# Feed-forward products of a two-block kernel: each weight tile loaded twice instead of three times, with two sums side by side in a PSUM bank

## The chip, the cores and the metric

The kernel runs on one core of a Trainium2 chip. The metric is the device time of one execution in microseconds (us); the figure used is the median of several runs. Engines are named as in the profile: TensorE (PE, its weight loads PEld), VectorE (DVE), ScalarE (ACT), GpSimd (POOL) and SyncE (SP), which issues the weight loads from memory.

## What is computed

Two transformer blocks run one after the other on 256 rows of 1024 features (the first block has 16 more rows, which no longer count when its feed-forward part begins). Both end in a feed-forward part, and these are what the change touches:

```python
# first block: gate and up are 1024 x 2816, down is 2816 x 1024
h = h + (jax.nn.silu(hn @ w_gate[l]) * (hn @ w_up[l])) @ w_down[l]
# second block: up is 1024 x 4096, down is 4096 x 1024
x = x + jnp.square(jax.nn.relu(h2 @ w_up[l])) @ w_down[l]
```

`hn` and `h2` are the RMS-normed rows. Everything is float32.

## The kernel before, in words

**Split numbers.** TensorE multiplies a reduced float format (fp32r) at full speed. To keep the accuracy, every operand x is held as two parts, the first x rounded to the format and the second the rest, x minus the first. A product is then three matmuls: first x first, first x second, and second x first. `three` (lines 524 to 530) issues them into one PSUM region. For weights as the stationary side these are three weight loads (a, a, b) and three streams of the rows (c, d, c).

**Pieces.** The weights come as a list of 251 pieces, most 128 x 1024 (512 KB), in the order of `PIECES`. SyncE loads piece i into one of five slots of `raw` as soon as piece i-5 has been split. ScalarE copies it into the first part (line 1320, `first_parts`), VectorE subtracts (line 1843, `second_parts`), and the two parts lie in one of six slots of `parts`, free again when TensorE has used the piece six before. This is called a split below.

**The order of VectorE and ScalarE.** All engines have one written order. `full` and `freed` (waits for a bank to be filled, or emptied) first call `keep_ahead`: before an engine waits for a bank, it does its share of the splits up to the fourth piece (`AHEAD = 4`) behind the last piece that went into this bank. So the splits stand between the waits for the banks, and a late wait makes all splits behind it late.

**First block's feed-forward part** (lines 913 to 926). For each of 22 feature tiles f, TensorE computes gate.f into columns 0 to 255 of a PSUM bank and up.f into columns 256 to 511 (`feature_product`, 8 weight tiles k of 128 features for each, 24 matmuls of 256 columns). One bank, `gu_f`, holds both; four banks take turns. After f = 0 it also multiplies out `rows2`, the inverse norms of the rows for all partitions, which wait for VectorE's `rms2`. After f = 5, 9, 13 and 17 it does four pieces of down (`down`, lines 863 to 902: 12 matmuls of 512 columns for each piece, into banks 4 to 7), and after f = 21 the last six, in two rounds, one for each tile of rows. VectorE (line 2135 on) multiplies the bank by the inverse norms into `gu` (line 2138) and then, in `hidden_rest`, waits for ScalarE's SiLU (line 1523), multiplies gate and up (2131), waits for ScalarE's copy into the first part of the hidden tile (1525), and subtracts for the second part (2133). down for tiles f-5 to f-2 waits for these.

**Second block's** (lines 1263 to 1276). 32 pieces of up, two to a bank (`up_j`, j = 0 to 15); from j = 3 on, after every second j, four pieces of down. ScalarE applies ReLU straight from the bank (line 1742) into one of four `relu2` slots, squares it into the first part (1744), and GpSimd squares again and subtracts (1811, 1813). VectorE has nothing but splits here, from the end of the norm (line 2544) to the last results (line 2550).

Of the kernel before, what the change touches and what calls it, by code (L numbers as in the profile page):

```python
# [150 lines left out]
def build(nc, consts, params, weights, x, meta, out, line_dram):  # L151
    ctx = ExitStack()
    with ctx:
# [137 lines left out]
        def release(ins, name):  # L291
            ins.then_inc(bank_free[jobs[name][0]], 1)
# [193 lines left out]
        def _(pe):  # L486
# [44 lines left out]

            arrivals = {}
# [16 lines left out]
            def feature_product(name, cols, ps, acts=hT, ahead_of={}):  # L549

                w = [half.rearrange("p (k n) -> p k n", k=KD) for half in split(name)]
                for k in range(KD):
                    if k in ahead_of:
                        ahead_of[k]()
                    need(k)
                    last = three(ps, [h[:, k, :] for h in w], [acts[:, s, k, cols] for s in range(2)],
                                 k == 0, k == KD - 1)
# [355 lines left out]
            for f in range(FT1):  # L913
                name = f"gu_{f}"
                ps = opened(name)
                done_with(f"gate.{f}", feature_product(f"gate.{f}", tok, ps[:, 0:SEQ],
                                                       ahead_of={4: lambda: first_rows(1)} if f == 0 else {}))
                if f == 0:
                    turn[0], turn[1] = 0, 4
                closed(feature_product(f"up1.{f}", tok, ps[:, SEQ:2 * SEQ]), name)  # L920
                piece_used[f"up1.{f}"] = name
# [341 lines left out]
            for n in range(8):  # L1263
                for j in (2 * n, 2 * n + 1):
                    name = f"up_{j}"
                    ps = opened(name)
                    done_with(f"up2.{2 * j}", feature_product(f"up2.{2 * j}", tok, ps[:, 0:SEQ],
                                                              ahead_of=late_rows if j == 0 else {}))
                    if j == 0:
                        turn[0], turn[1] = 0, 4  # L1270
                    closed(feature_product(f"up2.{2 * j + 1}", tok, ps[:, SEQ:2 * SEQ]), name)
                    piece_used[f"up2.{2 * j + 1}"] = name
# [30 lines left out]
        def _(act):  # L1303
# [216 lines left out]
            for f in range(FT1):  # L1520
                full(act, f"gu_{f}")
                freed(act, f"gu_{f}")
# [213 lines left out]
            for j in range(FT2 // 2):  # L1736
                name = f"up_{j}"
                full(act, name)
                if j >= 4:

                    act.wait_ge(sem("hidden2"), j - 3)
                release(A(relu2[:, j % 4, :], bank_of(name), ACT.Relu), name)
                freed(act, name)
# [74 lines left out]
        def _(dve):  # L1818
# [317 lines left out]
            for f in range(FT1):  # L2136
                full(dve, f"gu_{f}")
# [587 lines left out]
```

## Time and profile before

| | |
|---|---|
| median of 3 runs | 939.38 us (938.78 to 940.14) |
| profiled execution | 939.0 us |
| its span, first to last instruction | 937.2 us |
| mean granted clock of TensorE | 0.996 |
| busy: TensorE, VectorE, ScalarE, GpSimd | 98%, 66%, 50%, 17% |
| first feed-forward part | about 153.7 to 343 us of the span |
| second feed-forward part | about 752 to 935 us |

The busy share of TensorE counts the time in which any matmul is under way. Matmuls overlap in the array (one of 256 columns lasts 0.28 us, but the next starts 0.12 us after it), so the cost of one is read from the distance between starts. A timeline row gives start, duration, engine, line, operation, tiles and count, and in brackets how long the engine was idle before it and for whom it waited.

### The profile page before, as it was taken

What the parts mean: (1) busy time and instruction counts of PE and PEld (TensorE: products, weight loads), DVE (VectorE), ACT (ScalarE), POOL (GpSimd) and SP (SyncE); (2) the same over time, 40 slices, a digit from 0 to 9 for tenths busy, and PEclk for the clock granted to TensorE, in tenths of its full rate; (3) what the DMA queues carried; (4) which work ended last, traced back from release to release, by engine and by line L of the source; (5) the groups of instructions that cost most, each with busy time, mean ns of one, the idle gap of its engine ahead of it and who ended that gap; (6) DMA issues with size and microseconds to landing.
All of it is one profiled execution on the core that took longest, in us unless ns stands there. A gap on an engine that the chain in (4) does not pass through costs nothing. (4 is left out here: it accounts for less than half of the span.)

```text
span 937.2 us, 17705 instructions
## 1 busy us (share of the span) xinstructions
PE 921.7 (98%) x6958; PEld 827.6 (88%) x6958; DVE 616.3 (66%) x1335; ACT 466.3 (50%) x925; POOL 155.3 (17%) x111
## 2 busy tenths in 40 slices
PE   9999999999999999999999999999999999999998
PEld 8898787999999989888988888998888899999996
DVE  4657767657556587799777878356775674555543
ACT  6555655545445364474444773354453464444441
POOL 1100000000000007002974214000000023332231
PEclk9999999999999999999999999999999999999999
DMA  6830343565556444655432101032746545555551
GB/s 246 265 130 1 101 142 117 166 217 179 181 181 218 161 156 156 222 178 188 152 117 86 46 14 69 3 115 69 237 138 208 180 138 201 180 181 191 192 179 45
DMA packets 38579, 139.31 MB, mean 149 GB/s; under 512 B 4326, under 2 KB 4582, under 8 KB 38497
## 3 DMA queue, kind: packets, MB, share of 16 engines
q1 hardware_dynamic: 37152, 134.10, 43.3%
q10 hardware_dynamic: 816, 2.25, 0.7%
q0 software_dynamic: 528, 1.84, 0.6%
q8 instruction: 55, 0.90, 0.4%
q14 instruction: 28, 0.22, 0.1%
HBM read 137.09 MB, written 1.08 MB: 147 GB/s over the span
## 5 line engine op out<-in xcount | busy, mean ns | idle before, releaser
L1843 DVE TENSOR_TENSOR parts<-raw,parts 128x1024 fp32r<-128x1024 f32 (+2 forms) x225 | 285.2, 1303 | 128.7 <-ACT parts L1320 123.8
L1320 ACT ACTIVATE parts<-raw 128x1024 fp32r<-128x1024 f32 (+2 forms) x225 | 228.1, 1050 | 117.5 <-PE psum L530 97.2
L528 PE MATMUL psum<-hT,parts 128*128 128x256 f32 (+1 forms) x928 | 263.9, 284 | 1.4 <-DVE hT L1860 1.2
L529 PE MATMUL psum<-hT,parts 128*128 128x256 f32 (+1 forms) x928 | 262.5, 283 | 0.0
L530 PE MATMUL psum<-hT,parts 128*128 128x256 f32 (+1 forms) x928 | 260.9, 281 | 0.0
L528 PEld LDWEIGHTS psum<-hT,parts 128*128 128x128 f32 x928 | 174.7, 188 | 5.0 <-issue 1.8
L530 PEld LDWEIGHTS psum<-hT,parts 128*128 128x128 f32 x928 | 176.0, 190 | 0.0
L529 PEld LDWEIGHTS psum<-hT,parts 128*128 128x128 f32 x928 | 175.0, 189 | 0.5
L528 PE MATMUL psum<-parts,arena_r 128*128 128x512 f32 x344 | 135.1, 393 | 0.9 <-DVE arena_r L1858 0.7
L530 PE MATMUL psum<-parts,arena_r 128*128 128x512 f32 x344 | 134.0, 390 | 0.0
L529 PE MATMUL psum<-parts,arena_r 128*128 128x512 f32 x344 | 133.9, 389 | 0.0
L1369 ACT ACTIVATE arena<-arena,npeaks 128x128 f32<-128x128 f32 (+4 forms) x136 | 55.9, 414 | 50.0 <-DVE npeaks L1921 20.1
L528 PEld LDWEIGHTS psum<-parts,arena_r 128*128 128x128 f32 x344 | 64.6, 188 | 14.6 <-DVE arena_r L1858 1.4
L530 PEld LDWEIGHTS psum<-parts,arena_r 128*128 128x128 f32 x344 | 64.6, 188 | 13.6
L529 PEld LDWEIGHTS psum<-parts,arena_r 128*128 128x128 f32 x344 | 64.6, 188 | 12.5
L528 PE MATMUL psum<-parts,hT 128*128 128x512 f32 (+1 forms) x176 | 69.2, 393 | 1.7 <-DVE peaks L1921 1.1
L1774 POOL TENSOR_SCALAR arena<-cbuf 128x256 f32<-128x256 f32 x16 | 16.8, 1049 | 320.5 <-DVE scr L2169 319.4
L529 PE MATMUL psum<-parts,hT 128*128 128x512 f32 (+1 forms) x176 | 68.1, 387 | 0.0
L530 PE MATMUL psum<-parts,hT 128*128 128x512 f32 (+1 forms) x176 | 68.0, 387 | 0.0
L1811 POOL TENSOR_TENSOR arena<-arena 128x512 f32<-128x512 f32 x16 | 17.2, 1073 | 284.1 <-ACT arena_r L1744 284.1
L1784 POOL TENSOR_TENSOR parts<-raw,parts 128x1024 fp32r<-128x1024 f32 x20 | 48.5, 2422 | 1.6
L647 PE MATMUL psum<-arena 128*128 128x128 f32 x288 | 40.1, 276 | 1.4 <-DVE arena L2336 1.0
(329 smaller groups left out, 1192.9 us busy)
## 6 DMA issues: line engine op xcount, KB each, us to landing
raw<-weights SPq DMA_DIRECT2D x247, 512.0 KB, 4.1
raw<-weights SPq DMA_DIRECT2D x4, 384.0 KB, 4.4
X<-x SPq DMA_DIRECT2D x2, 512.0 KB, 5.2
out<-X SPq DMA_DIRECT2D x2, 512.0 KB, 2.6
arena<-lines POOLq DMA_DIRECT2D x1, 768.0 KB, 9.8
cbuf<-consts ACTq DMA_DIRECT2D x1, 561.0 KB, 6.5
arena<-lines POOLq DMA_DIRECT2D x1, 544.0 KB, 5.9
arena<-params ACTq DMA_DIRECT2D x1, 512.0 KB, 6.5
```

Of the source, the lines that this page charges most:

```text
L528: mm(ps, a, c, start=start, stop=False)
L529: mm(ps, a, d, start=False, stop=False)
L530: return mm(ps, b, c, start=False, stop=stop)
L647: last = mm(o, flat[:, at:at + P], vt[t], start=(t == 0 and not g["meta"]), stop=(t == g["tiles"] - 1))
L1320: signal(A(split_slot(name)[0], whole_piece, ACT.Copy), "first_parts")
L1369: signal(A(map_slot(g, E, n), map_slot(g, S, n), ACT.Exp, bias=npeaks[:, col:col + 1], scale=-1.0 if negated else 1.0, accum_out=sums[:, c ...
L1774: nc.gpsimd.tensor_scalar(al[:, h, :], cst("negdist"), slope, None, ALU.mult).then_inc(sem("alibi"), 1)
L1784: nc.gpsimd.tensor_tensor(second, whole_piece, first.bitcast(F32), ALU.subtract)\
L1811: nc.gpsimd.tensor_tensor(v, v, v, ALU.mult).then_inc(sem("squares2"), 1)
L1843: signal(V_.tensor_tensor(second, whole_piece, first.bitcast(F32), ALU.subtract), "split_vector")
```

## The change

`side_by_side` replaces `three` where the region given is a whole bank of 512 columns. The stationary side is the first part of the weights once, with both parts of the rows as one moving operand (512 columns, two sums side by side), and the second part of the weights once, with the first part of the rows (256 columns, added to the left sum). The wanted product is the sum of the two halves. Each gate, up1 and up2 piece now fills a bank of its own. In the first block VectorE adds the halves of each bank with a reduction over groups of two (step 256) into `gu`, and then multiplies by the inverse norms there. In the second block VectorE adds them into `relu2`, and ScalarE's ReLU works in place. Down and all other products stay as they are. The waits follow: ScalarE waits for `rows_scaled` instead of the bank, and the slot of `relu2` is waited for by VectorE.

```diff
+            def side_by_side(ps, stationary, moving, start, stop):
+
+                a, b = stationary
+                two_sums = ps.rearrange("p (s n) -> p s n", s=2)
+                if start:
+                    mm(two_sums, a, moving, start=True, stop=False)
+                    return mm(ps[:, 0:SEQ], b, moving[:, 0, :], start=False, stop=False)
+                mm(ps[:, 0:SEQ], b, moving[:, 0, :], start=False, stop=False)
+                return mm(two_sums, a, moving, start=False, stop=stop)
...
-                    last = three(ps, [h[:, k, :] for h in w], [acts[:, s, k, cols] for s in range(2)],
-                                 k == 0, k == KD - 1)
+                    if ps.shape[-1] == 2 * SEQ:
+                        last = side_by_side(ps, [h[:, k, :] for h in w], acts[:, :, k, cols], k == 0, k == KD - 1)
+                    else:
+                        last = three(ps, [h[:, k, :] for h in w], [acts[:, s, k, cols] for s in range(2)],
+                                     k == 0, k == KD - 1)
...
             for f in range(FT1):
-                name = f"gu_{f}"
-                ps = opened(name)
-                done_with(f"gate.{f}", feature_product(f"gate.{f}", tok, ps[:, 0:SEQ],
-                                                       ahead_of={4: lambda: first_rows(1)} if f == 0 else {}))
-                if f == 0:
-                    turn[0], turn[1] = 0, 4
-                closed(feature_product(f"up1.{f}", tok, ps[:, SEQ:2 * SEQ]), name)
-                piece_used[f"up1.{f}"] = name
+                for w, piece in enumerate((f"gate.{f}", f"up1.{f}")):
+                    name = f"gu{w}_{f}"
+                    ps = opened(name)
+                    closed(feature_product(piece, tok, ps,
+                                           ahead_of={4: lambda: first_rows(1)} if f == w == 0 else {}), name)
+                    piece_used[piece] = name
+                    if f == w == 0:
+                        turn[0], turn[1] = 0, 4
...
-                full(act, f"gu_{f}")
-                freed(act, f"gu_{f}")
+                full(act, f"gu1_{f}")
+                act.wait_ge(sem("rows_scaled"), f + 1)
...
             for j in range(FT2 // 2):
-                name = f"up_{j}"
-                full(act, name)
-                if j >= 4:
-
-                    act.wait_ge(sem("hidden2"), j - 3)
-                release(A(relu2[:, j % 4, :], bank_of(name), ACT.Relu), name)
-                freed(act, name)
+                full(act, f"up1_{j}")
+                freed(act, f"up0_{j}")
+                freed(act, f"up1_{j}")
+                signal(A(relu2[:, j % 4, :], relu2[:, j % 4, :], ACT.Relu), "relu2")
+                act.wait_ge(sem("relu2"), j + 1)
...
             for f in range(FT1):
-                full(dve, f"gu_{f}")
-                release(V_.tensor_tensor(ffn1["gu"].rearrange("p (s n) -> p s n", s=4)[:, f % 4, :], bank_of(f"gu_{f}"),
-                                         ffn1["rows"], ALU.mult), f"gu_{f}")
+                for w in range(2):
+                    name = f"gu{w}_{f}"
+                    full(dve, name)
+                    release(V_.tensor_reduce(gu[:, f % 4, w, :], bank_of(name).rearrange("p (s n) -> p n s", s=2), AXX,
+                                             ALU.add), name)
+                freed(dve, f"gu0_{f}")
+                freed(dve, f"gu1_{f}")
+                both_rows = ffn1["gu"].rearrange("p (s n) -> p s n", s=4)[:, f % 4, :]
+                signal(V_.tensor_tensor(both_rows, both_rows, ffn1["rows"], ALU.mult), "rows_scaled")
                 hidden_rest(f)
...
+            for j in range(FT2 // 2):
+                for w in range(2):
+                    name = f"up{w}_{j}"
+                    full(dve, name)
+                    if j >= 4 and w == 0:
+                        dve.wait_ge(sem("hidden2"), j - 3)
+                    release(V_.tensor_reduce(relu2[:, j % 4, SEQ * w:SEQ * w + SEQ],
+                                             bank_of(name).rearrange("p (s n) -> p n s", s=2), AXX, ALU.add), name)
```

The part of TensorE's loop over the second block's pieces changes as the first block's does, with banks `up0_j` and `up1_j` in place of `up_j`.

## Rows read from the trace of the kernel before

**Rows 1.** The page, part 1: busy time, share of the span, instructions.

```profile
PE 921.7 (98%) x6958; PEld 827.6 (88%) x6958; DVE 616.3 (66%) x1335; ACT 466.3 (50%) x925; POOL 155.3 (17%) x111
```

**Rows 2.** Windows inside both feed-forward parts: length, engines' busy time, clock, DMA.

```profile
162.99:202.40 39.41, 39.41 (x291) 37.57 (x290) 27.21 (x34) 21.42 (x30) 0.00 (x0) 1.00 0.58 185
202.40:236.10 33.70, 33.70 (x242) 31.82 (x241) 20.43 (x24) 15.07 (x20) 0.00 (x0) 1.00 0.58 193
760.00:788.50 28.50, 28.50 (x198) 26.63 (x197) 20.27 (x20) 15.60 (x19) 13.33 (x8) 1.00 0.58 186
788.50:910.00 121.50, 121.50 (x806) 112.11 (x805) 61.32 (x43) 56.15 (x65) 34.77 (x22) 1.00 0.57 186
```

**Rows 3.** Groups of TensorE by form: busy us, mean ns, idle before.

```profile
L528 PE MATMUL psum<-parts,arena_r 128*128 128x512 f32 x344 | 135.1, 393 | 0.9 <-DVE arena_r L1858 0.7
L528 PE MATMUL psum<-parts,hT 128*128 128x512 f32 x152 | 61.0, 401 | 0.6 <-DVE parts L1843 0.3 <-DVE hT L2181 0.2
```

**Rows 4.** Timeline of ScalarE, two of its copies during down pieces.

```profile
233.74 1.06 ACT L1320 ACTIVATE parts<-raw 128x1024 fp32r<-128x1024 f32 x1 [1.66 <-PE psum L530]
236.46 1.06 ACT L1320 ACTIVATE parts<-raw 128x1024 fp32r<-128x1024 f32 x1 [1.66 <-PE psum L530]
```

**Rows 5.** Timeline of VectorE, one steady gate/up pair.

```profile
247.81 0.69 DVE L2138 TENSOR_TENSOR arena<-psum,arena 128x512 f32<-128x512 f32 x1 [0.25 <-PE psum L530]
249.04 0.43 DVE L2131 TENSOR_TENSOR arena<-arena 128x256 f32<-128x256 f32 x1 [0.54 <-ACT arena L1523]
250.90 2.36 DVE L1843 TENSOR_TENSOR parts<-raw,parts 128x1024 fp32r<-128x1024 f32 x2 [0.52 <-ACT parts L1320]
253.51 0.69 DVE L2138 TENSOR_TENSOR arena<-psum,arena 128x512 f32<-128x512 f32 x1 [0.25 <-PE psum L530]
```

**Rows 6.** Timeline of VectorE at the first pairs of the first block.

```profile
163.97 0.69 DVE L2138 TENSOR_TENSOR arena<-psum,arena 128x512 f32<-128x512 f32 x1 [0.23 <-ACT arena L1518]
...
168.34 2.36 DVE L1843 TENSOR_TENSOR parts<-raw,parts 128x1024 fp32r<-128x1024 f32 x2 [0.53 <-ACT parts L1320]
170.61 0.69 DVE L2138 TENSOR_TENSOR arena<-psum,arena 128x512 f32<-128x512 f32 x1
...
173.70 2.36 DVE L1843 TENSOR_TENSOR parts<-raw,parts 128x1024 fp32r<-128x1024 f32 x2 [0.53 <-ACT parts L1320]
175.98 0.68 DVE L2138 TENSOR_TENSOR arena<-psum,arena 128x512 f32<-128x512 f32 x1
```

**Rows 7.** Groups of VectorE by form.

```profile
L2138 DVE TENSOR_TENSOR arena<-psum,arena 128x512 f32<-128x512 f32 x22 | 15.2, 690 | 16.5 <-PE psum L530 16.3 <-ACT arena L1518 0.2
...
L2151 DVE TENSOR_TENSOR arena<-X,arena 128x512 f32<-128x512 f32 x4 | 2.8, 692 | 0.1
...
L2292 DVE TENSOR_REDUCE st<-arena 128x16 f32<-128x1024 f32 x1 | 1.2, 1214 | 0.0
```

**Rows 8.** Timeline of VectorE at the end of the first block.

```profile
326.63 0.69 DVE L2138 TENSOR_TENSOR arena<-psum,arena 128x512 f32<-128x512 f32 x1 [0.25 <-PE psum L530]
...
330.06 2.36 DVE L1843 TENSOR_TENSOR parts<-raw,parts 128x1024 fp32r<-128x1024 f32 x2 [0.58 <-ACT parts L1320]
...
334.61 0.68 DVE L1901 TENSOR_TENSOR X<-psum,X 128x512 f32<-128x512 f32 x1
335.33 0.69 DVE L2151 TENSOR_TENSOR arena<-X,arena 128x512 f32<-128x512 f32 x1
```

**Rows 9.** Timeline of TensorE, the first matmul of gate.1.

```profile
162.99 0.36 PE L528 MATMUL psum<-hT,parts 128*128 128x256 f32 x1
```

**Rows 10.** Timelines of ScalarE, VectorE and GpSimd, start of the second block.

```profile
760.70 0.60 ACT L1742 ACTIVATE arena<-psum 128x512 f32<-128x512 f32 x1 [0.93 <-PE psum L530]
...
777.82 0.60 ACT L1742 ACTIVATE arena<-psum 128x512 f32<-128x512 f32 x1 [2.54 <-PE psum L530]
...
762.95 3.96 DVE L1843 TENSOR_TENSOR parts<-raw,parts 128x1024 fp32r<-128x1024 f32 x2 [0.24 <-ACT parts L1320]
...
763.68 2.15 POOL L1813 TENSOR_TENSOR arena_r<-arena,arena_r 128x512 fp32r<-128x512 f32 x1
```

More of the change, by code:

```diff
@@ L1264, in _ @@
                 for j in (2 * n, 2 * n + 1):
-                    name = f"up_{j}"
[L1266 to L1272, printed above, removed]
+                    for w in range(2):
+                        name = f"up{w}_{j}"
+                        piece = f"up2.{2 * j + w}"
+                        ps = opened(name)
+                        closed(feature_product(piece, tok, ps, ahead_of=late_rows if j == w == 0 else {}), name)
+                        piece_used[piece] = name
+                        if j == w == 0:
+                            turn[0], turn[1] = 0, 4
                 if n >= 1:
@@ L1736, in _ @@
             for j in range(FT2 // 2):
-                name = f"up_{j}"
-                full(act, name)
-                if j >= 4:
-                    act.wait_ge(sem("hidden2"), j - 3)
-                release(A(relu2[:, j % 4, :], bank_of(name), ACT.Relu), name)
-                freed(act, name)
+                full(act, f"up1_{j}")
[3 more added lines that the diff above has]
+                act.wait_ge(sem("relu2"), j + 1)
                 signal(A(a2[:, 0, 2 * j:2 * j + 2, :], relu2[:, j % 4, :], ACT.Square), "hidden2_first")
@@ L2544, in _ @@
             link(V_.tensor_tensor(st[:, 10:12], st[:, 4:6], st[:, 4:6], ALU.mult))
+            for j in range(FT2 // 2):
+                for w in range(2):
+                    name = f"up{w}_{j}"
+                    full(dve, name)
[3 more added lines that the diff above has]
+                                             bank_of(name).rearrange("p (s n) -> p n s", s=2), AXX, ALU.add), name)
             for t in range(TT):
```

## The prediction, as it was made before the changed kernel ran

> **What bounds the kernel now.** I read the busy shares and slices of the page first, then the matmul groups by form, then, for the stretches that the change touches, the timelines of VectorE and ScalarE. TensorE is busy 98% of the span, VectorE 66% [rows 1]. Both feed-forward stretches show TensorE busy without a gap, with a granted clock of 1.00, its 2.4 GHz level [rows 2], so a cheaper stream of matmuls shortens the span, unless another engine then sets the pace.
>
> What a matmul costs is its distance to the next. A gate/up pair (48 matmuls of 256 columns) takes 5.70 us: two VectorE products that each waited for TensorE stand at 247.81 and 253.51 [rows 5], so 118.8 ns each, where 256 columns at 2.4 GHz are 106.7. One down piece (12 matmuls of 512) takes 2.72 us, from the two splits on ScalarE that wait for TensorE at 233.74 and 236.46 [rows 4]: 226.7 ns for 213.3 of columns. A matmul with its weights thus costs about 12 to 13 ns beside its columns, wide or narrow.
>
> VectorE has hardly any room in a gate/up pair. There it does two splits (128x1024), one product (512) and two small ones (256) with two waits for ScalarE between them; the steady pair of 5.70 us has 0.25 us of waiting for TensorE in it [rows 5]. In the first pairs of the first block it starts late and never waits for TensorE: 170.61 to 175.98 is a pair of 5.37 us [rows 6].
>
> **The change part by part.** *Matmuls.* Per weight tile k three matmuls of 256 become one of 512 and one of 256: 356.3 becomes 226.7 + 118.8 = 345.5 ns, 10.8 less. There are 44 + 32 pieces of 8 tiles, 608 in all: 6.6 us; per pair 0.17 (5.70 to 5.53). The bounds: the 512-wide matmuls whose stationary side is hT are longer in the list (401 against 393 ns [rows 3]); 8 ns more on each would leave 1.7 us of the 6.6. Here the stationary side is `parts`, so I take 226.7. The upper bound is a switch of weights that costs nothing behind a wide matmul: 12 ns more on each of 608, 7 us; every narrow and wide row carries the same extra, so I don't expect it. The Trainium skill ("TensorE: Matmul & The Clock Gate", Back-to-back issue gap) gives N/2.4 + 2.5 ns for the gap; by that a matmul less is worth 2.5 ns and the whole edit 1.5 us. The trace disagrees with it: 12 ns, so its rule is not in my sum.
>
> *VectorE, first block.* Each pair gains two reductions of 512 elements from PSUM, and the product with the rows stays, now from SBUF and behind its own engine's semaphores. The trace has no reduction with groups of two and a step of 256 between the two. Nearest: 512 elements take 690 ns from PSUM and 692 from SBUF, and a reduction of 1024 with long groups 1214 ns [rows 7], that is 1.02 ns for each further element, the rate of the other operations. I take 0.69. The lower bound is the 256-wide operation, as if only the outputs counted (0.42 [rows 5]; each 0.27 less per reduction takes 0.54 from VectorE's pair, and the first and the last wait below all but vanish: 3 us more gained). The upper bound is each element counting twice, the 1024-wide row (1.22). Back to back a 512-wide operation occupies 0.60 (the next starts before its end), behind a wait on itself 0.72 (334.61 to 335.33 [rows 8]). VectorE's pair becomes 5.37 + 0.60 + 0.72 = 6.69 us, against 5.53 of TensorE. It falls back 1.16 us in every pair and catches up only while TensorE works on the four down pieces (10.88 us, in which VectorE has four splits of 1.14 to do). A cycle of four pairs and four down pieces is 31.3 us for VectorE and 33.0 for TensorE, so it catches up wholly, if nothing overflows before.
>
> Does it overflow? VectorE's order is written: it splits the piece four ahead of the bank's last piece before it waits for that bank. Call R(f) the start of the emptying of gate.f.
> At the start: TensorE waits for the inverse rows and starts gate.1 at 162.99 as now [rows 9]. VectorE's first product stands at 163.97 because ScalarE's copy of the rows ends then; two reductions come ahead of it, 1.32 later. The split at 168.34 moves to 169.66 and R(1) is 170.80. R(4) = 190.87, R(5) = 197.56. TensorE ends up.5 at 162.99 + 5 x 5.53 = 190.64. The banks (four, reused after four pieces) are just free: gate.5 wants bank 2 at 185.1, emptied at R(3) + 0.75 = 184.9. Split down.0 stands ahead of R(4), ready 191.0 (0.3 late); split down.2 ahead of R(5), ready 197.7, wanted at 191.0 + 5.44 = 196.4 (1.2 late); split gate.6 follows the whole of step 5, R(5) + 0.60 + 1.14 + 0.72 + 3.09 + 1.23 = 204.3, wanted 203.1 (1.2 late). Now gate.6 starts at 162.99 + 5 x 5.70 + 10.88 = 202.4. So the first six pairs end 1.9 us later than now, and how fast the matmuls are does not matter there.
> In the middle, pairs 6 to 21: nothing is late, 16 x 0.17 = 2.8 us gained.
> At the end pairs 18 to 21 run without down pieces; R(18) can stand 3.0 after gate.18 starts (its 2.77 and the end of the last matmul), R(21) 20.1 later, and the split of down.20, which stands behind step 21, is ready at 23.1 + 5.55 + 1.23 = 29.8. TensorE wants it at 4 x 5.53 + 4 x 1.36 = 27.6: 2.2 us of waiting. Now that split ends at about 331.2 [rows 8], 4.6 after the product of 326.63, and TensorE wants it 5.4 after. First block: 1.9 - 2.8 + 2.2 = 1.3 us longer. ScalarE's SiLU, copy and splits only move with VectorE.
>
> *Second block.* VectorE gets two reductions per pair; the ReLU reads SBUF instead of PSUM (a 128x512 row either way), the square and GpSimd's two operations keep their order. Here VectorE had only splits, about 2.3 us per pair, lengthened by GpSimd (two take 3.96 at 762.95 [rows 10]). A new chain arises: ReLU behind the second reduction, then square, then ScalarE's next split, then VectorE's: 760.70 to 762.95 now [rows 10], so 2.25. VectorE's pair: 1.14 + 0.60 + 1.14 + 0.72 + 2.25 = 5.9, and up to 7.0 with GpSimd's 1.1, against 5.53. From 761.5 on (where the norm's chain ends now) the first pair brings VectorE to 766.2, three more to 783.8 or, at 7.0 each, to 787.2, and the split of up2.8 is ready between 785.0 and 789.4; TensorE wants it at 788.0 in the new pace and has it at 788.5 in the old (777.82 + 10.88, less ScalarE's 0.2 behind the last matmul [rows 10]). I count these four pairs as no gain. The other 12 have down pieces between them (VectorE 19 us of 22) and gain 12 x 0.17 = 2.1 us. ReLU slots, hidden tiles and the end of the block have a pair and more to spare.
>
> **Sum.** 1.3 - 2.1 = -0.8 us on the profiled execution's 939.0 us (span 937.2): 938.2. The median of the runs shown is 0.4 above that execution, so 938.6. About 0.2% (1.9 us) is what a measurement of this kernel can tell from no change; my forecast lies within it.
>
> **The rivals.** *A, the reduction is slow.* Its two operands lie 256 words apart, so every read jumps. By the upper bound (1.22, back to back 1.14, behind a wait 1.25) VectorE's pair is 7.76 us and R(1) 171.9. Then gate.6 is split at 171.9 + 4 x 7.76 + 7.8 = 210.7, 8.3 later than it starts now; a cycle (4 x 7.76 + 4 x 1.14 = 35.6) is 1.9 longer than TensorE's present one (33.7), three times, 5.7; at the end down.20's split comes 4.4 + 3 x 7.76 + 7.8 = 35.5 after gate.18, wanted after 28.3 in the present pace, 7.2; in the second block four pairs make up2.8 4.4 late, less the 2.1, 2.3. Together 23.5, 962 us; half way, at 0.95 us, 950. It decides from about 0.90 us on, where VectorE's cycle passes TensorE's. For it: no row has a jump at each element. Against it: VectorE's forms cost their element count alone [rows 7]. The Trainium skill has both: "Advanced Engine Details and Errata", PSUM Cachelines, wants every two consecutive elements adjacent; "Vector Engine (DVE) Microarchitecture Reference", Measured stream behaviour on trn2, has 1.73 ns per element for a two-source operation that jumps every element (an estimate of 1.04 us for this one, 954 us), but the full rate for a one-source operation that alternates between two regions of SBUF and writes one word for two read, which is the shape of this one. No row here shows either. Chance 0.25: 950 us, 944 to 962.
> *B, VectorE keeps up.* If my three waits don't arise (TensorE's pieces are buffered deeper than I count, or VectorE's waits for ScalarE shrink when it is late), the 6.6 us come in, less the first pair of each block, where TensorE waits for the norm: 933.3. For it: VectorE is busy only 50 to 71% of these stretches [rows 2]. Against it: the written order, and the 5.37 us pair that had no wait for TensorE. Chance 0.12.
> *C, the saving per matmul is mostly absent* (1.7 us or less of it): of the 28 pairs that I count as gained each brings 0.04 instead of 0.17, and the last wait shrinks by as much: 941; inside my own range.
>
> **How the numbers follow.** Forecast 0.63, A 0.25, B 0.12. The forecast's own range is 936.0 to 942. The range has to take in part of A: 936.0 to 955 leaves out about 0.11 below (B) and 0.09 above. Faster by over 0.2% (under 937.5): B and 0.06 of the forecast, 0.18. Within: 0.44. Slower (over 941.3): A, and 0.13 of the forecast, 0.38.
>
> **What would show it.** Reductions of 0.69 us on VectorE, 76 of them. Pairs of 5.53 us in the middle of both blocks. VectorE's pair at 6.7 us from 171 to 197, no wait for TensorE in it; TensorE waiting for VectorE's splits (line of the subtraction) about 2.7 us in all before gate.6 and 2.2 at the last down pieces, nowhere else over 1 us. The forecast is wrong if a reduction takes over 0.90 us, if waits for splits appear in the cycles 6 to 17, or if there are none at all.

## The result, and the profile after

| | before | after |
|---|---|---|
| median of the runs on one chip (5 each) | 940.14 us (938.78 to 941.30) | 949.46 us (947.20 to 951.52) |
| profiled execution, its span | 939.0, 937.2 us | 949.46, 947.6 us |
| mean granted clock of TensorE | 0.996 | 0.994 |

The change makes the kernel slower: 1.0096 times the time before, 95% interval 1.0081 to 1.0111. The forecast was 938.6 us and no measurable change. 949.5 lies inside the stated range (936 to 955), but outside the forecast's own (936.0 to 942). That it lies inside is luck: the range reached so far up for the slow reduction of rival A, and the reductions were not slow.

The page of the changed kernel, part 1, stands against [rows 1]:

```profile
PE 924.7 (98%) x6350; PEld 799.7 (84%) x6350; DVE 656.1 (69%) x1411; ACT 465.3 (49%) x925; POOL 154.5 (16%) x111
```

TensorE issues 608 matmuls and 608 weight loads fewer, as written. It is nevertheless busy 3 us longer, and the span has grown by 10.4 us. VectorE has 76 more operations and 40 us more work.

The windows of the changed kernel (length, busy time of PE, PEld, DVE, ACT and POOL with counts, PEclk, DMA share, GB/s) stand against [rows 2]; two short ones are added:

```profile
162.99:202.40 39.41, 37.77 (x195) 32.30 (x196) 28.93 (x41) 16.03 (x24) 0.00 (x0) 0.96 0.46 137
165.54:168.90 3.36, 3.36 (x12) 2.88 (x12) 1.43 (x3) 1.70 (x2) 0.00 (x0) 0.50 0.36 138
339.60:343.00 3.40, 3.40 (x9) 2.62 (x9) 2.83 (x4) 0.90 (x1) 0.00 (x0) 0.50 0.81 258
788.50:910.00 121.50, 121.50 (x607) 102.64 (x606) 77.58 (x69) 59.98 (x70) 38.44 (x24) 1.00 0.56 194
```

In the first window TensorE now has gaps (37.77 of 39.41 us busy), and its clock is 0.96. The two short windows are stretches at the 1.2 GHz level (0.50), one right after each of the two long waits below. In the last window the engine has no gap and the full clock, as before.

To say where the time went, I compare the start of the same work on TensorE in both traces (after less before, us of the span):

| point | after less before | added since the row above |
|---|---|---|
| first feed-forward part begins (same code up to here) | +0.6 | +0.6 |
| gate.6 begins | +3.8 | +3.2 |
| pairs 6 to 21 done | +3.7 | -0.1 |
| down of the first block done | +8.9 | +5.2 |
| before the products of the compressed keys, about 388 us | +9.9 | +1.0 |
| second feed-forward part begins | +10.6 | +0.7 |
| end | +10.4 | -0.2 |

So two places cost 8.4 us between them, and the 5 us that the forecast expected from cheaper matmuls in the middle and in the second block did not come. The 0.6, 1.0 and 0.7 lie in code that the change does not touch. The 1.0 comes and goes without it: e6, which is the kernel before with one buffer moved, has 1.5 us there.

**The first place: gate.1.** Timeline of TensorE of the changed kernel (start, duration, engine, line, operation, tiles; in brackets the idle time and for whom it waited):

```profile
163.16 0.71 PE L917 MATMUL psum<-cbuf,st 128*128 128x128 f32 x4 [0.70 <-DVE st L1886]
165.34 0.68 PE L537 MATMUL psum<-hT,parts 128*128 128x512 f32 x1 [1.47 <-DVE arena L2151]
165.82 0.41 PE L538 MATMUL psum<-hT,parts 128*128 128x256 f32 x1
166.04 0.41 PE L539 MATMUL psum<-hT,parts 128*128 128x256 f32 x1
166.25 0.63 PE L540 MATMUL psum<-hT,parts 128*128 128x512 f32 x1
166.68 0.41 PE L539 MATMUL psum<-hT,parts 128*128 128x256 f32 x1
```

The first matmul of gate.1 waits 1.47 us for a reduction of VectorE (line 2151). gate.0 was put into bank 2, where the rotation stood. Then the rotation is reset, up.0 gets bank 0, `rows2` bank 1, and gate.1 bank 2 again, before VectorE has emptied it. The half clock follows: the wide matmul of 166.25 has its successor 0.43 us later, where at full clock it is 0.23. From the first matmul of gate.1 to that of gate.6 the changed kernel takes 1.5 us more than before.

**The second place: down.20.** Timelines of TensorE and VectorE of the changed kernel:

```profile
335.38 0.39 PE L530 MATMUL psum<-parts,arena_r 128*128 128x512 f32 x1
339.12 0.47 PE L528 MATMUL psum<-parts,arena_r 128*128 128x512 f32 x1 [3.35 <-DVE parts L1854]
339.42 0.49 PE L529 MATMUL psum<-parts,arena_r 128*128 128x512 f32 x1
339.72 0.63 PE L530 MATMUL psum<-parts,arena_r 128*128 128x512 f32 x1
340.14 0.63 PE L528 MATMUL psum<-parts,arena_r 128*128 128x512 f32 x1
```

```profile
310.40 0.69 DVE L2151 TENSOR_REDUCE arena<-psum 128x256 f32<-128x512 f32 x1 [0.90 <-PE psum L540]
...
313.25 0.69 DVE L2151 TENSOR_REDUCE arena<-psum 128x256 f32<-128x512 f32 x1 [1.03 <-PE psum L540]
...
318.29 0.68 DVE L2151 TENSOR_REDUCE arena<-psum 128x256 f32<-128x512 f32 x1
...
320.81 0.69 DVE L2156 TENSOR_TENSOR arena<-arena 128x512 f32<-128x512 f32 x1
322.04 0.43 DVE L2142 TENSOR_TENSOR arena<-arena 128x256 f32<-128x256 f32 x1 [0.55 <-ACT arena L1536]
322.95 0.42 DVE L2144 TENSOR_TENSOR arena_r<-arena,arena_r 128x256 fp32r<-128x256 f32 x1 [0.48 <-ACT arena_r L1538]
323.90 1.23 DVE L1854 TENSOR_TENSOR parts<-raw,parts 128x1024 fp32r<-128x1024 f32 x1 [0.53 <-ACT parts L1333]
325.05 0.68 DVE L2151 TENSOR_REDUCE arena<-psum 128x256 f32<-128x512 f32 x1
...
335.84 0.42 DVE L2142 TENSOR_TENSOR arena<-arena 128x256 f32<-128x256 f32 x1 [0.82 <-ACT arena L1536]
...
337.75 2.36 DVE L1854 TENSOR_TENSOR parts<-raw,parts 128x1024 fp32r<-128x1024 f32 x2 [0.58 <-ACT parts L1333]
```

In pairs 18 to 21, without down pieces between them, VectorE needs 6.76 us a pair (318.29 to 325.05) and TensorE 5.7. No operation of that pair waits for TensorE, and the waits for ScalarE in it (0.55, 0.48, 0.53) are those of the pair before the change (0.54, 0.48, 0.52 or 0.53; two of them in [rows 5]): the pair is longer by VectorE's own added operations. The split of down.20 starts at 337.75 and lets TensorE go on at 339.12; before the change it was ready at about 331.2 [rows 8].

**The middle.** The changed kernel's matmuls within one piece (the distance between starts is the cost):

```profile
274.03 0.28 PE L539 MATMUL psum<-hT,parts 128*128 128x256 f32 x1
274.15 0.40 PE L540 MATMUL psum<-hT,parts 128*128 128x512 f32 x1
274.39 0.28 PE L539 MATMUL psum<-hT,parts 128*128 128x256 f32 x1
274.50 0.39 PE L540 MATMUL psum<-hT,parts 128*128 128x512 f32 x1
274.73 0.28 PE L539 MATMUL psum<-hT,parts 128*128 128x256 f32 x1
...
275.90 0.42 PE L540 MATMUL psum<-hT,parts 128*128 128x512 f32 x1
276.15 0.29 PE L539 MATMUL psum<-hT,parts 128*128 128x256 f32 x1
```

The narrow matmul costs 0.11 to 0.12 us. The wide ones cost 0.24, 0.23 and 0.25. Over the pieces of 225 to 292 us the medians for the wide one are 231, 228, 256 and 233 ns as k goes up, repeating every four k, 237 on average; the narrow one is at 119.5. A weight tile costs 356.4 ns (2853 a piece), and before it cost 356.5. Of the 10.8 ns a tile that the forecast counted on, 0.1 came.

### The profile page after: what moved, and what is told of

Its sections match the earlier page's. It is cut to its first block and busy times, and to the rows that moved or that the text cites. A ratio compares the mean times of both kernels' runs of the same rounds, so it can differ in the third digit from the quotient of the medians.

```text
span 947.6 us, 16642 instructions
## 1 busy us (share of the span) xinstructions
PE 924.7 (98%) x6350; PEld 799.7 (84%) x6350; DVE 656.1 (69%) x1411; ACT 465.3 (49%) x925; POOL 154.5 (16%) x111
## 5 line engine op out<-in xcount | busy, mean ns | idle before, releaser
L1854 DVE TENSOR_TENSOR parts<-raw,parts 128x1024 fp32r<-128x1024 f32 (+2 forms) x225 | 280.2, 1275 | 85.9 <-ACT parts L1333 80.3
L540 PE MATMUL psum<-hT,parts 128*128 128x512 f32 x532 | 194.6, 402 | 0.0
L539 PE MATMUL psum<-hT,parts 128*128 128x256 f32 x532 | 151.2, 284 | 1.2 <-DVE hT L1871 1.2
L540 PEld LDWEIGHTS psum<-hT,parts 128*128 128x128 f32 x532 | 101.2, 190 | 22.5
L539 PEld LDWEIGHTS psum<-hT,parts 128*128 128x128 f32 x532 | 100.9, 190 | 5.6 <-DVE hT L1871 1.7
L528 PE MATMUL psum<-hT,parts 128*128 128x256 f32 (+1 forms) x320 | 92.7, 290 | 0.2 <-DVE parts L1854 0.2
L529 PE MATMUL psum<-hT,parts 128*128 128x256 f32 (+1 forms) x320 | 91.2, 285 | 0.0
L530 PE MATMUL psum<-hT,parts 128*128 128x256 f32 (+1 forms) x320 | 90.7, 283 | 0.0
L528 PEld LDWEIGHTS psum<-hT,parts 128*128 128x128 f32 x320 | 60.8, 190 | 2.9 <-issue 1.8
```

Of the source, the lines that this page charges most:

```text
L528: mm(ps, a, c, start=start, stop=False)
L529: mm(ps, a, d, start=False, stop=False)
L530: return mm(ps, b, c, start=False, stop=stop)
L539: mm(ps[:, 0:SEQ], b, moving[:, 0, :], start=False, stop=False)
L540: return mm(two_sums, a, moving, start=False, stop=stop)
L1854: signal(V_.tensor_tensor(second, whole_piece, first.bitcast(F32), ALU.subtract), "split_vector")
```

## The experiments

Ratios are against runs of the kernel before on the same chip, with 95% intervals.

**e1_narrow: the wide matmul taken apart again.** Does the saved weight load bring anything?

```diff
                 mm(ps[:, 0:SEQ], b, moving[:, 0, :], start=False, stop=False)
-                return mm(two_sums, a, moving, start=False, stop=stop)
+                if stop:
+                    return mm(two_sums, a, moving, start=False, stop=True)
+                mm(ps[:, 0:SEQ], a, moving[:, 0, :], start=False, stop=False)
+                return mm(ps[:, SEQ:2 * SEQ], a, moving[:, 1, :], start=False, stop=False)
```

> Changed kernel, but in 6 of the 8 weight tiles of each gate, up1 and up2 piece (k = 1 to 6) the 512-wide matmul is issued as two of 256, so the first part of the weights is loaded twice again: three loads as before, the sum the same. Theory (the wide matmul is worth no more than two narrow ones here; in the changed kernel it costs 228 to 256 ns by k, 238 on average, and two narrow ones of the kernel before cost 117.8 + 121): a gate/up pair stays at 5.70 us and the time at the changed kernel's, 949.5 +- 1.5. Rival (a saved load does bring the 10.9 ns per tile that the prediction took, and something else of the change eats it): pairs of 5.83 us, 456 x 10.9 ns = 5 us more, 954.5.

Measured: 947.81 us, ratio 1.0073 (1.0057 to 1.0088), 1.7 us under the changed kernel's 949.46 (the intervals of the two ratios overlap), where the rival had 5 us more. The bank wait, the wait at down.20 and both stretches at half clock are there again. A piece costs 2833 ns where the changed kernel's costs 2853: each of the six tiles taken apart became some 3 ns cheaper, and 76 pieces of 20 ns are 1.5 us. As the kernel stands, one wide matmul thus costs slightly more than two narrow ones with a load of their own. Why it does, this run does not say; e7 does.

**e2_bank: another rotation.** up.0 goes into bank 3, so that gate.1 does not meet bank 2.

```diff
                     if f == w == 0:
-                        turn[0], turn[1] = 0, 4
+                        turn[0], turn[1] = 3, 4
...
+            turn[0] = 44
             down("down1", FT1 - 6, 6, "d1", FT1, aT, hidden1, first_tile_turned)
```

> Changed kernel, but the banks of the first block's loop are taken from bank 3 on instead of bank 0 on, so that gate.1 doesn't take bank 2, which holds gate.0 until VectorE has emptied it (the bank of the later stages is set back to what it was). Theory (TensorE waits 1.5 us at gate.1 for that bank, and the wait brings a stretch of 3.4 us at half clock, 1.5 us more; without it VectorE, whose pair takes 6.76 us against 5.70, is what TensorE meets next): no wait at gate.1 and no half clock there, but waits for splits between down.0 and gate.6, whose start goes from 206.3 to about 205.4 (when VectorE has split it); about 1 us gained, 948.5. Rival (VectorE is not late enough for that): the whole 3.2 us come back, 946.3, gate.6 at 203.1.

Measured: 947.28 us, 1.0069 (1.0054 to 1.0084), between the two expectations; the trace decides between them. The wait at gate.1 and the half clock behind it are gone. In their place come waits for VectorE's splits at down.2 and gate.6. Timeline of TensorE of e2:

```profile
197.71 0.50 PE L528 MATMUL psum<-parts,arena_r 128*128 128x512 f32 x1 [0.90 <-DVE parts L1855]
204.57 0.47 PE L537 MATMUL psum<-hT,parts 128*128 128x512 f32 x1 [1.11 <-DVE parts L1855]
```

These are the waits that the prediction had worked out (1.2 and 1.2). The changed kernel hid them behind its bank wait. The changed kernel's bank wait is thus real, but little is to be had by taking it away, since VectorE's lateness lies right behind it: from the start of the part to gate.6 e2 loses 2.4 us against the kernel before, and the changed kernel 3.2. The rest of the 2.2 us between e2 and the changed kernel lies in code that they share (in the traces 1.0 us before the part begins and 0.9 ahead of the compressed keys).

**e3_early: the splits of down.20 and down.21 ahead of step 21.**

```diff
+                if f == FT1 - 1:
+                    second_parts(INDEX[f"down1.{f}"] + 1)
                 freed(dve, f"gu0_{f}")
                 freed(dve, f"gu1_{f}")
```

(The same on ScalarE, and the rotation set to 22 for what comes later.)

> Changed kernel, but in the last step of the first block (f = 21) both engines do their shares of the splits of down.20 and down.21 ahead of the product with the rows and the SiLU, instead of behind the whole step; the banks of the later stages are counted on from 22, as in the kernel before. Theory (TensorE waits 3.5 us for the split of down.20, and loses 1.7 us more in the 3.4 us at half clock that follow): both gone, 5.2 us gained, 944.3. Rival (the hidden tile 21 or the norm's chain, now 2.3 us later on VectorE, take its place): a new wait of 1 to 3 us before down.21 or before the norm's products, 946 to 949. And if the later banks matter, the 0.9 us longer wait before the compressed keys (about 388 us) goes too, else not.

Measured: 950.23 us, 1.0094 (1.0078 to 1.0111): nothing gained. The wait for the split turns into one for the last hidden tile. Timeline of TensorE of e3:

```profile
341.34 0.53 PE L528 MATMUL psum<-parts,arena_r 128*128 128x512 f32 x1 [1.86 <-DVE arena_r L2147]
```

Half clock follows this wait too. The stage costs 3.8 us more than before, where the changed kernel's costs 5.2, and the new rotation adds 1.6 us of bank wait at the start of the second block. One operation put first makes another late: what is late there is VectorE's whole queue.

**e4_pair512: both parts of a row tile stored as one run of 512 words.**

```diff
+        hF = hT[:, :, :, :].rearrange("p s k n -> p (s k n)")[:, 0:2 * KD * SEQ].rearrange("p (k s n) -> p s k n", s=2, k=KD)
...
-                    closed(feature_product(piece, tok, ps,
+                    closed(feature_product(piece, tok, ps, acts=hF,
```

> Changed kernel, but the rows of both feed-forward parts lie in hT so that the two parts of a feature tile k are side by side (512 words in one run, starting every 2 KB, instead of two runs of 256 that lie 8704 bytes apart and start every 1088 bytes). Theory (the wide matmul's cost goes by where its rows lie: 231, 228, 256, 233 ns for k mod 4 = 0 to 3 in the changed kernel): 227 ns for each k, and the narrow one 117 for each: a pair of 5.50 us; 3.2 us gained in pairs 6 to 21, 2.5 in the second block, and the wait at down.20 takes some 0.5 of it back: 944. Rival (a moving operand from hT costs 6 ns more whatever its place): pairs of 5.60, 946.5. Third (no effect of layout): 949.5.

Measured: 946.37 us, 1.0059 (1.0043 to 1.0076). The wide matmuls come out at 229 to 240 ns, 234 on average, without the 256; a weight tile at 352. It lies between the two expectations and pointed on: in down, 512 columns of `parts` as the moving side take 227. `hT` starts at byte 100704 of a partition, an odd multiple of 32, and `parts`, by the sizes declared between the two, at a multiple of 128.

**e5_second_only: the change in the second block alone.** (The hunks of the first block left out.)

> The kernel before with the change made in the second feed-forward block alone. Theory (the saved weight load is worth nothing, and the loss sits at two places of the first block: the bank wait and half clock at gate.1, 3 us, and the late splits, their wait and half clock at the end of the first block, 5 us): the time of before within 1.5 us, 939 to 941.5, second block within 0.5 us of before's (its k tile about 356 ns). Rival (the change costs or gains something in the second block that the traces hide, such as VectorE arriving late at the down pieces there): more than 2 us from before, either way.

Measured: 942.54 us, 1.0024 (1.0013 to 1.0036), 1 us above the expectation. In the trace there is one new wait at the beginning of the second feed-forward part. Timeline of TensorE of e5:

```profile
765.48 0.50 PE L537 MATMUL psum<-hT,parts 128*128 128x512 f32 x1 [1.61 <-DVE arena L2562]
```

up_0's first bank is 1, the reset gives the third sum bank 1 again: the same mistake as at gate.1, and here only because the first block leaves the rotation elsewhere. A stretch of 3.4 us at half clock at 483 us accounts for 1.7 us more of the profiled execution. From 777 us to the end the second part runs 0.1 us faster than before. So the second part gains nothing, and loses nothing but this bank wait, which the fully changed kernel does not have; that kernel's loss is in the first block.

**e6_before_moved: the kernel before, with `hT` on a boundary.** One declaration moves; no instruction changes.

```diff
+        scr = sb("scr", [P, 514])
         hT = sb("hT", [P, 2, KD, ALL], F32R)
...
-        scr = sb("scr", [P, 514])
```

> The kernel before with one SBUF buffer (scr, 2056 bytes a partition) declared ahead of hT and not behind it, so that hT starts at a multiple of 64 and 128 bytes in its partition (102784) instead of at an odd multiple of 32 (100704); arena_r keeps its place; no instruction changes. Theory (a moving operand off a 64-byte boundary costs 3 to 6 ns a matmul): the three 256-wide matmuls of a k tile fall from 117.8, 121 and 117.8 ns, the 512-wide ones on hT from about 233 to 227; over the 608 weight tiles of the feed-forward blocks alone 1 to 6 us less, 934 to 939. Rival (the place in SBUF is nothing to TensorE): same time within 0.7 us and the same pitches.

Measured: 939.91 us, 0.9991 (0.9979 to 1.0003). The weight tile falls from 356.5 to 355.0 ns, which over 608 tiles is 0.9 us. The expectation of 3 to 6 ns for each matmul was too high: 256-wide matmuls hardly feel the place. Down's matmuls, neither of whose operands moves, meanwhile cost 227.6 ns instead of 226.8, which takes nearly the same back. The 0.7 us by which the median is lower are not clear of noise.

**e7_after_moved: the changed kernel, with the same move.**

> The changed kernel with the same move of scr ahead of hT. Theory (place): the two-run matmuls fall from 231, 228, 256 and 233 ns by k mod 4 toward 227 in all, the k tile from 356 to 345 ns; the middle and the second block gain 3 to 5 us, 944 to 947, while VectorE's splits become the limit in the first block. Rival 1 (the two runs of 256 words cost it, not where they start): the pattern by k stays and the time stays at 949 to 950. Rival 2 (only the outlier at one k in four goes): k tile 350 ns, 947 to 948.

Measured: 945.69 us, 1.0062 (1.0044 to 1.0081). Timeline of TensorE of e7, one piece up to k = 4:

```profile
271.10 0.39 PE L537 MATMUL psum<-hT,parts 128*128 128x512 f32 x1
271.33 0.28 PE L538 MATMUL psum<-hT,parts 128*128 128x256 f32 x1
271.44 0.28 PE L539 MATMUL psum<-hT,parts 128*128 128x256 f32 x1
271.56 0.39 PE L540 MATMUL psum<-hT,parts 128*128 128x512 f32 x1
271.78 0.28 PE L539 MATMUL psum<-hT,parts 128*128 128x256 f32 x1
271.90 0.40 PE L540 MATMUL psum<-hT,parts 128*128 128x512 f32 x1
272.13 0.28 PE L539 MATMUL psum<-hT,parts 128*128 128x256 f32 x1
```

The wide matmul now costs 0.22 to 0.23 us at nearly every k (medians 226 to 235), the piece 2780 ns, the weight tile 347.5: 9 ns less than in the kernel before. From 624 us to 911 us the kernel gains 2.2 us, 0.1 of it ahead of the second part, so that the part has the 2.1 of the forecast, and pairs 6 to 21 gain 2.2. This settles the missing saving. The other side grows at the same time. The window of e7 behind its wait:

```profile
335.88:341.00 5.12, 5.12 (x12) 4.07 (x13) 4.13 (x5) 1.56 (x3) 0.00 (x0) 0.51 0.74 244
```

and the waits of its TensorE (us in total, times, longest):

```profile
PE psum L528 <- DVE parts L1854: 4.5, 3, 3.7
...
PE psum L537 <- DVE parts L1854: 1.1, 1, 1.1
```

TensorE is faster, so VectorE is late by more: 3.7 us at down.20, and 1.1 at gate.6. The clock fell to half within the wait and stays there for 5 us behind it.

**e8_pair_moved: e4's layout and the move together.**

> The changed kernel with both rows of parts stored as one run of 512 words for each k (as e4) and with the move of scr ahead of hT. Theory (place and runs both cost): 512-wide at 227, narrow 117.8, k tile 345 ns as the forecast had it; against e4 (946.4) 2 us less in the second block and up to 1 us in the first, where VectorE is then late at the down pieces: 943 to 945.5. Rival (the 234 ns of e4 is the price of this matmul wherever the rows lie): no different from e4, 946 to 947.

Measured: 945.01 us, 1.0056 (1.0037 to 1.0075), pieces of 2812 and 2777 ns in turn, a weight tile of 349.3. The expected 345 is not reached, and in time e7 and e8 can't be told apart. The wide matmul stays where e4 had it, 234 ns on average: in this layout the move brings 2 to 3 ns a tile, nearly all of it in the narrow one, where with the kernel's own layout it brought 9. So the start of `hT` is not all that counts, and what else does, no run shows. With `hT` in place, two runs of 256 words cost nothing over one of 512.

**e9_half_read: a lighter VectorE in the first block.** The sum of the right half of each bank is left out.

```diff
-                    release(V_.tensor_reduce(gu[:, f % 4, w, :], bank_of(name).rearrange("p (s n) -> p n s", s=2), AXX,
-                                             ALU.add), name)
+                    release(V_.tensor_tensor(gu[:, f % 4, w, :], bank_of(name)[:, 0:SEQ], ffn1["rows"][:, SEQ * w:SEQ * w + SEQ],
+                                             ALU.mult), name)
...
-                signal(V_.tensor_tensor(both_rows, both_rows, ffn1["rows"], ALU.mult), "rows_scaled")
```

> e7 (the changed kernel, hT moved to a 128-byte boundary) with VectorE's three operations on a first-block pair (two reductions of 0.68 us and the product of 0.69 us) replaced by two products of 256 words that read the left half of each bank alone: the right half's sum is left out, TensorE's work is unchanged. Theory (the losses of the first block are VectorE's pair of 6.76 us, which falls to some 5.6 us): the wait of about 3.5 us at down.20 and the bank and split waits at gate.1, down.2 and gate.6 shrink to under 0.5 us in all and the half-clock stretch after the end goes with its wait; 940 to 941 goes to e7's 945.7 less 5 to 8 us: 937.5 to 940.5. Rival (the wait at the end is the pair's new chain through ScalarE, not VectorE's load): the end wait stays above 2 us, 943 to 946.

Measured: 938.82 us, 0.9982 (0.9970 to 0.9994), 6.9 us below e7 with the same work on TensorE (the kernel before measured the same on both chips, 940.66 and 940.62). Timeline of VectorE of e9, one pair from its second product to the next:

```profile
247.44 0.43 DVE L2152 TENSOR_TENSOR arena<-psum,arena 128x256 f32<-128x256 f32 x1
250.39 1.23 DVE L1855 TENSOR_TENSOR parts<-raw,parts 128x1024 fp32r<-128x1024 f32 x1 [0.52 <-ACT parts L1333]
251.54 0.42 DVE L2152 TENSOR_TENSOR arena<-psum,arena 128x256 f32<-128x256 f32 x1
253.00 0.42 DVE L2152 TENSOR_TENSOR arena<-psum,arena 128x256 f32<-128x256 f32 x1
```

VectorE's pair is 5.56 us, TensorE's pace. The wait at down.20 and the stretch at half clock behind it are gone, and gate.6 begins 1.7 us earlier than in e7. The bank wait at gate.1 is left, against the expectation, since one step of VectorE still stands ahead of it. Timeline of TensorE of e9:

```profile
164.13 0.50 PE L537 MATMUL psum<-hT,parts 128*128 128x512 f32 x1 [1.21 <-DVE arena L2152]
```

So it was VectorE's three operations, 2.05 us a pair, that cost the first block its gain and more. The edit shortens the way from the bank to ScalarE's SiLU as well, but in the changed kernel VectorE's waits for ScalarE were no longer than before (the rows of 322.04 to 323.90 above), so that way is not what made the pair long.

**e10_second_moved: the kernel before, `hT` moved, the change in the second block alone, its rotation reset to 2.**

```diff
                         if j == w == 0:
-                            turn[0], turn[1] = 0, 4
+                            turn[0], turn[1] = 2, 4
```

> The kernel before with hT moved (as e6), the change in the second feed-forward block alone (as e5), and the bank rotation there reset so that the first four sums fall in banks 1, 2, 3, 0 (e5 had 1, 0, 1, 2 and waited 1.5 us). Theory: e6's 939.9 less 256 weight tiles of about 7.5 to 8.5 ns, 2.0 us: 937.5 to 938.3, ratio 0.997. Rival (what the two-run matmul saves is given back at waits as in the first block): 939.5 to 941.

Measured: 938.52 us, 0.9980 (0.9969 to 0.9991). From 624 to 911 us it gains 2.2 us on the kernel before, without a bank wait. (The profiled execution has a stretch of 6.8 us at half clock at 17 us, in code that all the kernels share.)

**e11_middle_too: e10, and the change in pairs 6 to 17 of the first block as well.** Pairs 0 to 5 and 18 to 21 keep the old form.

```diff
+                if 6 <= f < 18:
+                    for w, piece in enumerate((f"gate.{f}", f"up1.{f}")):
+                        name = f"gu{w}_{f}"
+                        ps = opened(name)
+                        closed(feature_product(piece, tok, ps), name)
+                        piece_used[piece] = name
+                else:
...
```

> e10 with the change also in pairs 6 to 17 of the first block; pairs 0 to 5 and 18 to 21, where no or few down pieces give VectorE time, stay as before. Theory: 192 more weight tiles of 8 ns, 1.5 us less than e10, with no wait over 1 us at the end of the first block: 936 to 937, ratio 0.9955. Rival (VectorE's 6.76 us pair leaves the splits late even in the middle and the end wait comes back): same as e10 or slower, 938 to 941.

Measured: 935.87 us (934.94 to 938.85), 0.9954 (0.9936 to 0.9972), the fastest of all, span 933.3. Windows of e11, pairs 6 to 9 with their down pieces, and the last pairs:

```profile
202.40:236.10 33.70, 33.70 (x182) 29.03 (x181) 23.06 (x31) 14.78 (x20) 0.00 (x0) 1.00 0.47 149
318.00:330.00 12.00, 12.00 (x82) 11.06 (x81) 8.12 (x11) 6.32 (x9) 0.00 (x0) 1.00 0.51 175
```

No gap, full clock. (In the second row, pairs 18 to 21 run up to 324.66 and the last down pieces from there on; down.20 begins just behind the row, at 330.1, and no wait for its split is among TensorE's waits of this trace.) Where down pieces lie between the pairs, VectorE's 6.76 us are hidden; the four pairs at the end, in the old form, leave no wait at down.20. The new form in the middle brings what was expected of it (1.5 us more than e10 from 202 to 326 us of the span) with `hT` in place; the same kernel without the move was not run, and the changed kernel's 0.1 ns a tile says that there was next to nothing to be had there.

**e12_after_64: `hT` at a multiple of 64 bytes and not of 128** (e7, with `pbuf` declared behind `hT` as well).

> e7 with pbuf moved behind hT as well, so that hT starts at 100928: a multiple of 64 bytes and not of 128. Theory (64 bytes are enough): k tile 347 to 348 ns as in e7, 945 to 946.5. Rival (it takes 128): wide matmuls by k back toward 231 to 256, k tile 352 to 356, 948 to 950.

Measured: 947.61 us, 1.0067 (1.0047 to 1.0086); the weight tile costs 348.3 ns (2787 a piece), wide matmuls 226 to 235. In the pitches 64 bytes are as good as 128 within 1 ns. The time is 1 us above what I expected; the profiled execution has one more stretch at half clock (at 165 us) than e7's, and the intervals of the two overlap.

## Why the prediction was wrong, point by point

By stages the forecast had +1.9 us (first six pairs), -2.8 (pairs 6 to 21), +2.2 (end of the first block) and -2.1 (second block). Measured were +3.2, -0.1, +5.2 and -0.2, and 2.3 us more in code that the change does not touch.

- *A matmul and a load less are worth 10.8 ns a weight tile.* Wrong in this kernel: 0.1 ns. It is the step that decided the middle and the second block, 5 us. The forecast took the price of a wide matmul, 226.7 ns, from down, where `parts` is the moving side, and used it for one that streams `hT`. It asked only whether the stationary side was the same kind, and the longer rows that it looked at [rows 3] have `hT` there. What made the difference was the place of the moving `hT`: with it on a 64- or 128-byte boundary (e7, e12) 8 to 9 ns come in. Rival C had this size (1.7 us or less left), but from those rows, which are about another side, so its hit was in part luck. The Trainium skill's "TensorE: Matmul & The Clock Gate", Back-to-back issue gap, has a formula by which, as an estimate, the matmul less is worth 2.5 ns, and calls it the gap of an isolated matmul, not that of a stream with weight loads. The runs show 0.1 ns with `hT` where it was, and 9 with it moved.
- *"The banks (four, reused after four pieces) are just free."* Wrong at one point: gate.0 sits in the bank that gate.1 gets after the reset. That is 1.5 us of waiting, with a half clock behind it. Most of it only took the place of waits for VectorE: by e2 it made the stage 0.8 us longer. The step counted the rotation from the reset and not from the bank in use before it.
- *The start: first six pairs 1.9 us late.* The mechanism was right, R(1) came at 171.50 (170.80 forecast, 0.6 of the difference being there before the part begins), the pair of VectorE is 6.76 us (6.69 forecast), and without the bank wait (e2) the waits stand where they were put, 0.9 and 1.1 us. The stage was then 2.4 us longer, for 1.9 forecast. In the changed kernel the bank wait had used the others up.
- *The middle cycles have room.* Right: no waits from pair 6 to pair 17, in any of these runs.
- *The end: 2.2 us for the split of down.20.* It was 3.35 us. R(18) came 3.05 us after gate.18 began, as forecast. But R(19) came 7.9 us after R(18) and not 6.7: after the down pieces VectorE is in time and has to wait for the end of up.18 (the 1.03 at 313.25), and this time is lost to it. The half clock behind the wait (1.7 us) stood in no step.
- *Reductions at 0.69 us.* Right: 76 at 0.68 (0.675 to 0.692), so rival A falls although the kernel came out slower. The Trainium skill's "Vector Engine (DVE) Microarchitecture Reference", Measured stream behaviour on trn2, has the full rate for one source that alternates between two regions of SBUF, and here it holds for PSUM as well. The Trainium skill's "Advanced Engine Details and Errata", PSUM Cachelines, wants every two consecutive elements adjacent for the best throughput, and this reduction, in which no two are, took no longer than the contiguous 0.69.
- *The second block gains 2.1 us.* 0.2 at first; 2.1 with `hT` moved. The terms about VectorE and ScalarE there held: no split was late.
- *The sign.* Slower had a chance of 0.38, 0.25 of it for the slow reduction. The waits were worked out one by one, yet nothing was put by for what a wait brings with it, and the gain was booked in full against them.

What stays open: the 1.0 us ahead of the compressed keys, which varied from 0 to 1.5 us among the kernels; why the half clock came after some waits and not after others; and why the wide matmul did not gain by the move in the layout of e4 and e8.

## What to carry to other kernels

Before counting on a cheaper stream of matmuls, take the price of one from a row with the same moving operand at the same place in SBUF, and try that operand on a 64-byte boundary (it brought 9 ns a weight tile in this layout, 2 to 3 in that of e8). Give work to a second engine only in the stretches where its queue has room: the same change cost 9 us when it was made everywhere, 5 with `hT` moved (e7), and with `hT` moved brought 4.7 (the move alone measured 0.7, not clear of noise) where down pieces lie between or VectorE has slack. When banks turn, count from the bank that is in use when the turn is reset.

## What the runs showed of the hardware

- A 512-wide fp32r matmul on a moving operand that starts at an odd multiple of 32 bytes takes 228 to 256 ns by its k (237 on average; the tiles lie 1088 bytes apart), the same with the operand at a multiple of 64 or of 128 bytes 226 to 235. For 256-wide ones the place makes 0.5 ns. With one run of 512 words every 2048 bytes the wide one took 234 ns on average at either start (e4, e8). That the address of `hT` and not, say, its neighbours matters is shown by e6, e7 and e12 alone, which move other small buffers with it, and in these three down's matmuls, whose operands stay in place, cost 0.8 to 1 ns more.
- Waits of TensorE of 1.5 us (gate.1) and 3.4 to 3.7 us (down.20) came with 3.4 us, twice 6.8 us, at the 1.2 GHz level in 11 of 14 cases, and so did the 1.9 us of e3; in the traces without such waits (e9, e10, e11) no such stretch lay there. A stretch of 3.4 us with TensorE busy costs 1.7. It is not certain to come: e7 and e8 had the wait at gate.1 without it, e4 the one at down.20, and the 1.6 us at the start of the second block (e3, e5) brought none. Nor does it need a wait over 1 us just ahead: every trace, that of the kernel before too, has such a stretch at 17 to 24 us or at 102 us, in code that all share.
